# Compression product as four 64x64 products, row maxima spread through memory, last product's end ordered by factor

## What is computed

```python
blocks = kv[:, idx] + pe[None, None, :, None, :]      # 15 blocks of 32 tokens, stride 16
hid = jax.nn.silu(jnp.einsum('bnlgd,ldh->bngh', blocks, w1))
return jnp.einsum('bngh,hd->bngd', hid, w2)           # for k and for v, 4 groups of 64
...
dlog = jnp.where(tril, b[..., :, None] - b[..., None, :] + ih[..., None, :], -jnp.inf)
m_t = jnp.maximum(inter, jnp.max(dlog, axis=-1))      # a running maximum per token and head
...
x = x + rmsnorm((jax.nn.silu(gate) * up) @ w_ffn_down[l], g_post_ffn[l])
```

## Time and profile before

| | |
|---|---|
| runs before | 1652.1 us median of 3 (1652.01 to 1652.5) |
| profiled execution, span from first to last instruction | 1650.4 us |
| around the span, to the median of the runs | 1.7 us |
| TensorE busy | 1351.8 us, 82% of the span |
| VectorE, ScalarE, GpSimd busy | 514.0, 188.6, 37.2 us |
| mean granted TensorE clock | 0.918 |
| mean DMA rate | 314 GB/s |

### The profile page before, as it was taken

One profiled execution on the slowest core, in us unless ns is written; L12 is line 12 of the kernel. 1 busy time (PEld: TensorE's weight loads), 2 busy tenths in 40 slices (PEclk: granted clock), 3 DMA queues, 4 the chain that ended last, 5 costly groups with the idle time before them and its releaser, 6 DMA issues. The chain is left out here.

```text
span 1650.4 us, 21139 instructions
## 1 busy us (share of the span) xinstructions
PE 1351.8 (82%) x8810; PEld 778.8 (47%) x8810; DVE 514.0 (31%) x1078; ACT 188.6 (11%) x496; POOL 37.2 (2%) x91
## 2 busy tenths in 40 slices
PE   9999676666656666865676679999999999999997
PEld 5553121221212111311121123688888999599953
DVE  3432111201101100110110110445545664467875
ACT  2321010000000000000000000214444000100000
POOL 1100000000000000000000000000000000000001
PEclk9999887888879777887878899999999999999999
DMA  9688999999999999999999999713342442444332
GB/s 398 273 326 366 430 430 430 432 428 434 431 426 434 430 431 432 430 429 431 432 430 426 434 432 426 298 68 118 114 168 108 170 182 68 191 154 153 126 135 95
DMA packets 31340, 517.98 MB, mean 314 GB/s; under 512 B 3504, under 2 KB 4528, under 8 KB 7216
## 3 DMA queue, kind: packets, MB, share of 16 engines
q1 hardware_dynamic: 29360, 514.01, 74.6%
q10 hardware_dynamic: 1920, 3.10, 0.6%
HBM read 515.53 MB, written 1.05 MB: 313 GB/s over the span
## 5 line engine op out<-in xcount | busy, mean ns | idle before, releaser
L1014 PE MATMUL ps<-ring,scr 128*32 128x512 f32 (+2 forms) x3106 | 475.5, 740 | 238.1 <-DMA ring<-in_experts 233.5
L1014 PEld LDWEIGHTS ps<-ring,scr 128*32 128x32 f32 (+1 forms) x3106 | 122.1, 134 | 566.6 <-issue 296.9
L1014 PE MATMUL ps<-turned_T,ring 128*128 128x128 f32 (+1 forms) x1760 | 245.2, 299 | 0.8 <-DVE turned_T L1849 0.8
L1014 PEld LDWEIGHTS ps<-turned_T,ring 128*128 128x128 f32 x1760 | 227.2, 192 | 14.2 <-issue 4.4
L1014 PE MATMUL ps<-scr 128*128 128x128 f32 (+11 forms) x892 | 166.0, 385 | 16.9 <-DVE scr L1978 12.2
L1014 PEld LDWEIGHTS ps<-scr 128*128 128x128 f32 (+4 forms) x892 | 93.6, 177 | 84.5 <-issue 46.0
L1014 PE MATMUL ps<-ring,turned_T 128*128 128x128 f32 (+3 forms) x512 | 128.7, 409 | 0.8 <-DMA ring<-in_w_in 0.8
L1014 PEld LDWEIGHTS ps<-ring,turned_T 128*128 128x128 f32 x512 | 82.2, 191 | 44.5 <-issue 31.3
L1981 DVE TENSOR_TENSOR x<-x,ps 128x512 f32<-128x512 f32 x60 | 41.3, 688 | 195.4 <-PE ps L1014 195.3
L1969 DVE SCALAR_TENSOR_TENSOR scr<-scr,ps 128x512 f32<-128x512 f32 x16 | 11.0, 688 | 291.1 <-PE ps L1014 291.1
L1967 DVE SCALAR_TENSOR_TENSOR scr<-scr,ps 128x512 f32<-128x512 f32 x16 | 11.0, 688 | 221.0 <-ACT scr L797 221.0
(11 more groups left out here) (316 smaller groups left out, 1031.2 us busy)
## 6 DMA issues: line engine op xcount, KB each, us to landing
ring<-in_experts SPq DMA_DIRECT2D x69, 4096.0 KB, 22.9
ring<-in_experts SPq DMA_DIRECT2D x48, 2048.0 KB, 21.0
ring<-in_w_ffn_in SPq DMA_DIRECT2D x11, 2048.0 KB, 7.8
ring<-in_w_merge SPq DMA_DIRECT2D x10, 2048.0 KB, 7.7
ring<-in_w_ffn_down SPq DMA_DIRECT2D x11, 1024.0 KB, 4.8
ring<-in_w_out SPq DMA_DIRECT2D x4, 2048.0 KB, 25.8
ring<-in_w_ml SPq DMA_DIRECT2D x4, 2048.0 KB, 7.8
ring<-in_w_nsa SPq DMA_DIRECT2D x4, 2048.0 KB, 8.0
```

The costliest lines, as they stand in the source:

```text
L1014: return pe.matmul(o, l, rr, start=start, stop=stop)
```

## The change

- **Compression.** VectorE now writes k and v twice, once with the first 16 position vectors added (`kvlo`) and once with the last 16 (`kvhi`), in `placed(b)`, which takes the place of ScalarE's copies. The operands are exchanged: 64 rows by 64 strided columns of `kv` (16 places of each of four groups) are the stationary operand, `w1`, 128 columns, is the moving one. Even tokens go to the upper 64 output partitions, odd ones to the lower, k to bank 0 and v to bank 1, so that four products in a row use four quarters of the array. ScalarE copies the sums to `cmpA`; two products with `both` (two 64x64 identities) turn them and add even to odd. They stand in the middle of `conv(0)`.
- **Maxima.** ScalarE writes `nMR` to a DRAM tensor `negM` and, once that has landed and the tanh is issued, reads it back into all 128 partitions (`negMB`, 512 KB). The product with ones, and TensorE's wait ahead of it, are gone. VectorE waits for `negMB` once, before the loop.
- **Order.** `merge_sums(GATES0, 0)` moves on VectorE from ahead of the compression's results to behind the copies to `stall`.
- **End.** The last three pairs of the last product are ordered by factor: q outside, n inside. Each bank is announced when its last product is done. VectorE finishes the pieces in another order, and the last two pieces go out as (1,1), (1,0).

```diff
@@ -367 +365,2 @@
-        negMd = E(4 * T, parts=4)
+        negMB = E(4 * T)
+        negMD = nc.dram_tensor("negM", (4, T), F32, kind="Internal").ap()
...
@@ -397,4 +396,4 @@
-        kvc = E2(5 * T, "p (g t) -> p g t", g=5)
-        hidb = E2(2)
-        hpre = E2(2 * 60, "p (m n) -> p m n", m=2)
-        hth = E2(2 * 60, "p (m n) -> p m n", m=2)
+        kvlo = E2(GROUPS * T)
+        kvhi = E2(GROUPS * T + CMP_STRIDE)
+        cmpA = E2(2 * P, "p (m n) -> p m n", m=2)
+        hth = E2(2 * 64, "p (m n) -> p m n", m=2)
...
@@ -628,2 +627,2 @@
-                for h in range(2):
-                    sp.wait_ge(x4_done, 4 + 2 * t + h + 1)
+                for n, h in enumerate((1, 0) if t else (0, 1)):
+                    sp.wait_ge(x4_done, 4 + 2 * t + n + 1)
@@ -873,4 +871,0 @@
-            for b in range(2):
-                act.wait_ge(kvc_ps, b + 1)
-                act.activation(kvc[:, 2 * b:2 * b + 2, :], bank[6 + b].rearrange("p (g t) -> p g t", g=2), ACT.Copy)\
-                   .then_inc(kvc_sb, 1)
@@ -879,2 +874,8 @@
-            act.wait_ge(hid_pre, 1)
-            act.activation(hth, hpre, ACT.Tanh, scale=0.5).then_inc(hid_th, 1)
+            act.wait_ge(st_sb, 1)
+            act.dma_start(negMD, nMR).then_inc(in_negM, 16)
+            act.wait_ge(cmp_ps, 1)
+            act.activation(cmpA, ps[:, 0:2, 0:P], ACT.Copy).then_inc(hid_pre, 1)
+            act.wait_ge(cmp_ps, 2)
+            act.activation(hth, ps[:, 0:2, P:P + 64], ACT.Tanh, scale=0.5).then_inc(hid_th, 1)
+            act.wait_ge(in_negM, 16)
+            act.dma_start(negMB, negMD.rearrange("h t -> (h t)").partition_broadcast(P)).then_inc(in_negM, 16)
@@ -1431,0 +1433 @@
+            both = const("both")
@@ -1456 +1458 @@
-                            ins = mm(bank[5][0:4, m * T:(m + 1) * T], const("both")[:, 48 + 4 * m:52 + 4 * m], gaT)
+                            ins = mm(bank[5][0:4, m * T:(m + 1) * T], both[:, 48 + 4 * m:52 + 4 * m], gaT)
@@ -1459 +1461 @@
-                            ins = mm(bank[4][:, T + u * 56:T + u * 56 + 56], gaT[:, u * P:(u + 1) * P], const("both"))
+                            ins = mm(bank[4][:, T + u * 56:T + u * 56 + 56], gaT[:, u * P:(u + 1) * P], both[:, 0:56])
@@ -1471 +1472,0 @@
-            pe.wait_ge(pe_sb, 1)
@@ -1474,7 +1475,10 @@
-            for l in range(CMP_L):
-                for m in range(2):
-                    ins = mm(bank[m][:, 0:75].rearrange("p (g n) -> p g n", g=5), w1[64 * m:64 * m + 64, l, :],
-                             kvc[64 * m:64 * m + 64, :, l:l + CMP_STRIDE * (N_CMP - 1) + 1:CMP_STRIDE],
-                             l == 0, l == CMP_L - 1)
-                    if l == 0 and m == 0:
-                        ins.then_inc(tfree[5], 1)
+            for i in range(CMP_STRIDE):
+                kv, at = (kvlo, 2 * i) if i < 8 else (kvhi, 2 * i - CMP_STRIDE)
+                for c in range(2):
+                    at0 = at + c + (CMP_STRIDE if i >= 8 else 0)
+                    for m in range(2):
+                        rows = slice(64 * m, 64 * m + 64)
+                        ins = mm(bank[m][64 * c:64 * c + 64, 0:P], kv[rows, at0:at0 + CMP_STRIDE * 63 + 1:CMP_STRIDE],
+                                 w1[rows, 2 * i + c, :], i == 0, i == CMP_STRIDE - 1)
+                        if i == 0 and c == 0 and m == 0:
+                            ins.then_inc(tfree[5], 1)
@@ -1483 +1487,6 @@
-            conv(0).then_inc(proj_ps, 1)
+            conv(0, range(4)).then_inc(tfree[2], 1)
+            pe.wait_ge(hid_pre, 1)
+            for m in range(2):
+                ins = mm(bank[m][:, P:P + 64], cmpA[:, m, :], both)
+            ins.then_inc(cmp_ps, 1)
+            conv(0, range(4, KC)).then_inc(proj_ps, 1)
@@ -1490,2 +1498,0 @@
-                    if n == 0 and t == 0:
-                        ins.then_inc(tfree[2], 1)
@@ -1557,5 +1563,0 @@
-                pe.wait_ge(proj_sb, g * 7 + 1)
-                pe.nop(nofuse=True)
-                pe.wait_ge(st_sb, 1)
-                mm(bank[7][:, T:2 * T], const("ones", 4), negMd[:, bass.ds(g * T, T)]).then_inc(d_ps, 1)
-
...
@@ -1765 +1767 @@
-            def ff_down(n):
+            def ff_down(n, qs):
@@ -1771,2 +1773,3 @@
-                r.arrived(s, 1)
-                for q, (l, rr) in enumerate(((a[0][0], w[:, 0, 0]), (a[0][1], w[:, 1, 0]), (ss[:, 1], tt[:, 1]),
+                if 0 in qs:
+                    r.arrived(s, 1)
+                factors = ((a[0][0], w[:, 0, 0]), (a[0][1], w[:, 1, 0]), (ss[:, 1], tt[:, 1]),
@@ -1774 +1777,3 @@
-                                             (a[1][1], tt[:, 3]))):
+                           (a[1][1], tt[:, 3]))
+                for q in qs:
+                    l, rr = factors[q]
@@ -1782 +1787 @@
-                    if q == 6 or n == HALF - 1 and q:
+                    if q == 6 and n < HALF - ENDS or n == HALF - 1 and q:
@@ -1809,2 +1814,5 @@
-            for n in range(HALF):
-                ff_down(n)
+            for n in range(HALF - ENDS):
+                ff_down(n, range(7))
+            for q in range(7):
+                for n in range(HALF - ENDS, HALF):
+                    ff_down(n, (q,))
...
@@ -2071,0 +2079,10 @@
+
+            def placed(b):
+
+                dve.wait_ge(kvc_ps, b + 1)
+                for kv, l0 in ((kvlo, 0), (kvhi, CMP_STRIDE)):
+                    ins = dve.tensor_tensor(kv[:, b * 512:(b + 1) * 512].rearrange("p (n l) -> p n l", l=CMP_STRIDE),
+                                            bank[6 + b].rearrange("p (n l) -> p n l", l=CMP_STRIDE),
+                                            peT[:, l0:l0 + CMP_STRIDE].unsqueeze(1).broadcast_to([P, 32, CMP_STRIDE]), ALU.add)
+                ins.then_inc(kvc_sb, 1)
+
@@ -2087,0 +2105 @@
+            placed(0)
@@ -2096,12 +2114,2 @@
-            chain(dve.tensor_scalar(nMR, MR, -1.0, None, ALU.mult))
-            dve.tensor_tensor(negMd.rearrange("p (h t) -> p h t", h=4), nMR.unsqueeze(1).broadcast_to([4, 4, T]),
-                              const("eye4", 4).unsqueeze(2).broadcast_to([4, 4, T]), ALU.mult).then_inc(st_sb, 1)
-            merge_sums(GATES0, 0)
-            dve.wait_ge(cmp_ps, 1)
-
-            for m in range(2):
-                chain(dve.tensor_copy(hidb[:, m:m + 1], bank[m][:, 60:61]))
-            for m in range(2):
-                ins = dve.tensor_scalar(hpre[:, m, :], bank[m][:, 0:60], hidb[:, m:m + 1], None, ALU.add)
-            ins.then_inc(hid_pre, 1)
-            dve.wait_ge(hid_pre, 1)
+            dve.tensor_scalar(nMR, MR, -1.0, None, ALU.mult).then_inc(st_sb, 1)
+            placed(1)
@@ -2109,5 +2117,5 @@
-            chain(dve.scalar_tensor_tensor(out=hth, in0=hth, scalar=1.0, in1=hpre, op0=ALU.add, op1=ALU.mult))
-            dve.tensor_scalar(hidk, hth[:, 0, :], 0.5, None, ALU.mult)
-            dve.tensor_scalar(hidv[:, :, 0:N_CMP], hth[:, 1, :].rearrange("p (g n) -> p g n", g=4), 0.5, None, ALU.mult)\
-               .then_inc(hid_sb, 1)
-            dve.wait_ge(cmp_ps, 3)
+            chain(dve.scalar_tensor_tensor(out=hth, in0=hth, scalar=1.0, in1=ps[:, 0:2, P:P + 64], op0=ALU.add, op1=ALU.mult))
+            hid = hth.rearrange("p m (g n) -> p m g n", g=4)[:, :, :, 0:N_CMP]
+            dve.tensor_scalar(hidk.rearrange("p (g n) -> p g n", g=4), hid[:, 0], 0.5, None, ALU.mult)
+            dve.tensor_scalar(hidv[:, :, 0:N_CMP], hid[:, 1], 0.5, None, ALU.mult).then_inc(hid_sb, 1)
+            dve.wait_ge(cmp_ps, 4)
@@ -2118 +2125,0 @@
-            dve.wait_ge(cmp_ps, 2)
@@ -2120,0 +2128 @@
+            merge_sums(GATES0, 0)
@@ -2150,0 +2159 @@
+            dve.wait_ge(in_negM, 32)
@@ -2175,3 +2184,2 @@
-                dve.wait_ge(d_ps, g + 1)
-                dve.tensor_tensor(tm[:, 0:T], bank[7][:, T:2 * T], causTz, ALU.add)
-                dve.tensor_tensor(tm[:, T:384], bank[7][:, T + P:2 * T], causT, ALU.add).then_inc(d_in, 1)
+                dve.tensor_tensor(tm[:, 0:T], negMB[:, bass.ds(g * T, T)], causTz, ALU.add)
+                dve.tensor_tensor(tm[:, T:384], negMB[:, bass.ds(g * T + P, P)], causT, ALU.add).then_inc(d_in, 1)
@@ -2411 +2419,2 @@
-            dve.wait_ge(ffo_ps, HALF)
+            ends = HALF - ENDS
+            dve.wait_ge(ffo_ps, ends + 1)
...
@@ -2431,0 +2441,5 @@
+            dve.wait_ge(ffo_ps, ends + 5)
+            total(v2F, bank[5], v2F)
+            total(yF[:, 1, 1, :], bank[3], v2F, ff_h)
+            dve.wait_ge(ff_h, 2 * FF_STEPS + 3)
+            gained_half(1)
@@ -2433,3 +2447,4 @@
-            for h in range(2):
-                dve.wait_ge(staged, 7 * GROUPS + h + 1)
-                finished(0, h)
+            dve.wait_ge(staged, 7 * GROUPS + 1)
+            finished(0, 0)
+            dve.wait_ge(ffo_ps, ends + 6)
+            total(yF[:, 1, 0, :], bank[6], v2F, ff_h)
@@ -2437,3 +2452,3 @@
-            for h in range(2):
-                o = slice(h * 512, (h + 1) * 512)
-                chain(dve.tensor_tensor(zF[1][:, o], yF[:, 1, h, :], grows[:, 2, o], ALU.mult))
+            gained_half(0)
```

(46 more changed lines are left out.)

## The result

The changed kernel takes 1643.91 us (median of 4 runs, 1643.78 to 1644.22) against 1652.23 us before: 8.3 us less. The ratio of the runs is 0.995, with a 95% interval of 0.9937 to 0.9962. The forecast was 1645.5 us, with a range of 1643.5 to 1648.1. The span fell from 1650.4 to 1642.0 us.

The account below looks back on a forecast made before the run. TensorE's own work was taken to bound the kernel from the compression to the last product, with a tail of other engines behind. Terms 2.8 + 2.5 + 1.3 = 6.6 us off the span gave 1645.5 us, range 1643.5 to 1648.1.

Parts of the forecast that it names:

- The products' price: Compression: 128 records at 42 ns in place of 67, 5.4 us in all, a gain of 3.1 us.
- The row halves' 109 ns: Compression: profiled price of a 128-column record on two row halves, read as hardly any overlap.
- The perfect quarter: Compression's lower bound: fourfold overlap of the whole-array price, 115 / 4 = 29 ns a record, 3.7 us in all.
- four strips at 39: Compression: 128-column record on four column strips, 39 ns, the nearest row, from which 42 ns was taken.
- B: Compression: quarters do not overlap across columns, 109 to 115 ns a record, 1654.1 to 1654.8 us; chance 0.06.
- C: Compression: quarters overlap only as the column halves, 77 ns a record, 9.9 us, 1650.0 us in all; chance 0.06.
- The cap: First group: the load of w_nsa lands at 1088.6, so the compression stage cannot give more than 3.7 us.
- Slack ahead of the products: Before the compression: VectorE's second placed pair ends at 1078.5, TensorE asks at 1078.93; 0.4 us, no wait.
- The spread: Group loop: removing the spreading product saves 0.62 us in each of four groups, -2.5 us, between -2.6 and 0.
- rival D: Group loop keeps its length: a wait takes the 0.62 us back in each group; 1648.0 us, chance 0.07.
- The end: VectorE ends 4.5 us behind E, the last product's end, in place of 5.84; -1.3 us, between -1.0 and -1.8.
- all my low ends: Whole kernel: lowest ends of the three terms together, 3.7 + 2.6 + 1.8 = 8.1 us off, 1644.0 us.

Follow-up runs that it names:

- the early load: Changed kernel with the slot of w_nsa released at the first product of the conv ahead of the compression; 1643.56 us (5 runs), ratio 0.9947.
- the compression alone: Kernel before with only the compression's part of the change, merge sums behind it included; 1649.50 us against 1652.35, ratio 0.9983.
- the merge sums back: Changed kernel with the merge sums back in their old place on VectorE, behind placed(1); 1644.11 us (4 runs).
- the maxima alone: Kernel before with only the maxima spread through memory; 1650.01 us (11 runs), ratio 0.9986.
- the 128-row spread: Kernel before with the spreading product taken over 128 rows, 124 of them zero, in place of 4; 1651.80 us (10 runs), ratio 0.9997.

## Why the prediction was right, point by point

**What bounds.** TensorE stayed busy through the groups (47.39 of 47.42 us), at 1.00 granted clock, and what was taken from it came off the run.

**The products' price** was the term mis-sized: 42 ns a record, measured 31. I leaned on rows that don't hold what I read in them. The row halves' 109 ns come from bursts of sixteen records, eight with 128 and eight with 256 columns. By shape, of the first burst in the kernel before:

```profile
L1014 PE MATMUL ps<-scr 64*128 64x256 f32 x8 | 1.2, 377 | 0.0
L1014 PE MATMUL ps<-scr 64*128 64x128 f32 x8 | 0.9, 296 | 0.0
```

That is 2.1 us, but the burst lasts 1.51 (1112.10 - 1110.59): time in which records of both shapes run stands in both rows. Per 128 columns the burst takes 63 ns (1.51 us for 24 times 128 columns), so its halves did overlap. The column halves' 77 ns come from bursts mixed in the same way. In a run of 128 alike, two halves cost 55 to 58. The perfect quarter, which I kept as the lower bound (29), came nearest; the row that I took, four strips at 39, did not. Rivals B and C lived on the misread rows. The stride, priced at nothing, costs 0.3 us.

**The cap** then decided. I had put the landing of `w_nsa` at 1088.6 and the most that the stage could give at 3.7 us. The load landed at 1088.25, TensorE waited 0.33 us, the stage gave 3.7. Without the cap the arithmetic (8.54 - 3.97 = 4.57 us, less 0.45 for the turning and the cut conv) says 4.1, and the early load shows 13.37 - 9.26 = 4.1. The products gave 1.4 us more than I forecast, and the cap kept 0.4 us of it back: the term came out at the bound that I had given it.

**Slack ahead of the products**: 0.4 us by my account, 0.64 measured. Nowhere did I note that this slack comes from another part, the removal of the diagonal step; the compression alone shows that it is what keeps the wait away.

**The spread**, 0.62 us a group, measured 0.83. I read a record's price from its own start to the next start and left out what its shape does to its neighbours. That is 0.8 us over four groups.

**No wait in its place** (rival D): right. VectorE began the loop at 1094.12 (forecast 1095.2), the swap's DMAs were issued at 1099.61, and TensorE asked for the halves at 1105.72. The broadcast took 5.6 us, not 7.1, where a wait shows its landing (1085.13 to 1090.76, with the merge sums back).

**The end**: 1.3 forecast, 1.1 measured. VectorE's part came out to the tenth (the sum began at E + 0.3). GpSimd's first step took 0.83 us, not 0.50. Both stand beside the same kind of VectorE step; now the step begins 0.09 us into it, where it began 0.41 us into it before (1644.14, less 1643.73), and it ends with it. The price was no constant, and I took it for one. VectorE's pair of steps before:

```profile
1643.73 1.42 DVE L2429 SCALAR_TENSOR_TENSOR x<-gains,rst,x 128x512 f32<-128x512 f32 x2 [0.45 <-POOL rst L642]
```

**Sum**: 6.6 forecast, 8.1 by the parts; the misses of 0.9 (products), 0.8 (spread) and -0.2 (end) add up. The time is inside the range, but not by much and in part by luck. 8.1 us is what all my low ends gave together, with other shares: the spread gave more than the most that I had allowed it (3.3 us against 2.6), and the end less than its most. The 0.3 us of scatter ahead of the compression then brought the time below the 1644.0 of these low ends, and it is inside for the half microsecond that I had left for the median.

## What to carry to other kernels

Price a packed shape by its stream divided by the parts in use, and check a row of mixed bursts against the time of the whole burst: rows by shape count overlap twice. In a long run of 128 alike records the loads hid even with a quarter of the array. Then look at once for what is late next, since a stage that shrinks meets its own loads: here 4.1 us were to be had and 3.7 came. A small product of an odd shape costs its neighbours too, and a step moved onto an engine with 0.6 us of slack works only as long as nothing else stands ahead of it, so measure parts of a change also alone before taking one of them elsewhere.

## What the runs showed of the hardware

- A 64x64 quarter of the array with 128 moving columns in float32 takes 105 ns a record, two quarters 55 (different rows and banks) or 58 (same rows and bank), four 31, at the full granted clock of 1.00. Reading the stationary operand at a stride of 16 lengthens one load from 133 to 200 ns and the record by 2.4 ns.
- A 4-row product between full ones costs 0.2 us more in itself than one of 128 rows, and 0.1 us more in each neighbour.
- A GpSimd step on 128x1 that begins inside a VectorE step with two 128x512 operands from SBUF ends 0.17 us behind that step's end (a root 0.42 us), and so takes 0.50 to 0.83 us in place of 0.30 (the root 0.84 to 0.96 in place of 0.56).
- The end of the program. In twelve of fourteen profiles the span ends about 2.5 us behind VectorE's last step; with the maxima alone and with the 128-row spread it ends 3.6 us behind. In these two, one packet of instructions is fetched within the last 15 us of the span, in the other twelve none. The DMA view of the last 3.4 us, of the two profiles with maxima alone and before:

```profile
DMA packets 274, 0.50 MB, mean 150 GB/s; under 512 B 32, under 2 KB 32, under 8 KB 273
## 3 DMA queue, kind: packets, MB, share of 16 engines
...
q14 instruction: 1, 0.01, 0.6%
```

```profile
DMA packets 288, 0.52 MB, mean 154 GB/s; under 512 B 32, under 2 KB 32, under 8 KB 288
## 3 DMA queue, kind: packets, MB, share of 16 engines
...
```

  That the fetch delays the end is not shown; no run moved one without the other. But 1.1 us of a total can hang on the program's length in this way, half of what that variant gained. All eleven runs of that variant show it: their spans are 2.2 us shorter than before at the median, where TensorE gained 3.3.
